# Five query tiles of the first attention split whole in scratch and placed by DMA, and the rotation of some tiles a tick or two earlier

## What is computed

```python
h = rms_norm(x, norm_mix_pre[l])
proj = h @ w_in[l]
qa, ka, va, qb, kb, vb = jnp.split(proj, SPLITS, axis=-1)
qa = apply_rope(rms_norm(qa.reshape(B, S, 8, 64), q_norm_a[l]), ang_axial)
ka = apply_rope(rms_norm(ka.reshape(B, S, 2, 64), k_norm_a[l]), ang_axial)
out_a = global_attention(qa, ka, va)            # every query sees every key
qb = apply_rope(qb.reshape(B, S, 8, 64), ang_1d)
kb = apply_rope(kb.reshape(B, S, 2, 64), ang_1d)
out_b = window_attention(qb, kb, vb, sink_b[l]) # three blocks of 128 keys, with a sink
# apply_rope: concatenate([x1 * cos - x2 * sin, x2 * cos + x1 * sin]) on the halves x1, x2 of a head
```

## Time and profile before

| | |
|---|---|
| median of three runs | 1161.18 us (1160.88 to 1161.55) |
| the profiled execution | 1164.91 us, its span 1163.1 us |
| TensorE's granted clock | 0.995 of full speed |
| PE busy | 1133.3 us (97% of the span) |
| DVE, ACT, POOL busy | 650.2, 503.0, 124.5 us |
| the attention of the first block (ticks 0 to 63) | about 43 to 175 us of the span |

### The profile page before, as it was taken

One profiled execution on the slowest core, in us unless ns is written; L12 is line 12 of the kernel. 1 busy time (PEld: TensorE's weight loads), 2 busy tenths in 40 slices (PEclk: granted clock), 3 DMA queues, 4 the chain that ended last, 5 costly groups with the idle time before them and its releaser, 6 DMA issues.

```text
span 1163.1 us, 15505 instructions
## 1 busy us (share of the span) xinstructions
PE 1133.3 (97%) x5560; PEld 936.3 (80%) x5560; DVE 650.2 (56%) x1085; ACT 503.0 (43%) x859; POOL 124.5 (11%) x143
## 2 busy tenths in 40 slices
PE   8999989999999999999999999999999999999997
PEld 6788767898888888888898887787888888888886
DVE  5888896966444444333378588563544444433333
ACT  5788885544223223222255458453322322332321
POOL 1476743000000000000000004200000000000000
PEclk8999999999999999999999999999999999999999
DMA  7321202213222222233223220032322222222312
GB/s 266 109 73 51 59 19 108 92 55 140 95 104 90 94 102 96 92 108 109 96 77 109 91 76 16 19 109 73 111 92 105 93 95 100 95 103 93 106 55 73
DMA packets 32515, 106.20 MB, mean 91 GB/s; under 512 B 4048, under 2 KB 6736, under 8 KB 32336
## 3 DMA queue, kind: packets, MB, share of 16 engines
q1 hardware_dynamic: 31712, 104.60, 25.5%
q10 hardware_dynamic: 752, 0.92, 0.3%
HBM read 100.78 MB, written 2.10 MB: 88 GB/s over the span
## 4 chain that ended last, share of the span: by engine, by line
PE 86%; DVE 6%; ACT 3%; POOL 2%; issue 2%; DMA 1%; ACTq 0%; SPq 0%; DVEq 0%; POOLq 0%
PE bank L502 24%; PE bank L504 24%; PE bank L503 23%; PE bank L1015 1%; PE bank L1005 1%; DVE wl L423 1%; PE bank L1088 1%; PE bank L963 1%; PE bank L964 1%; PE bank L965 1%; POOL pr L1335 1%; PE bank L1090 1%; PE bank L1089 1%; PE bank L2004 1%; PE bank L2002 1%
## 5 line engine op out<-in xcount | busy, mean ns | idle before, releaser
L423 DVE TENSOR_TENSOR wl<-raw,wh 128x1024 fp32r<-128x1024 f32 x181 | 223.9, 1238 | 299.3 <-ACT wh L415 299.2
L415 ACT ACTIVATE wh<-raw 128x1024 fp32r<-128x1024 f32 x181 | 191.1, 1057 | 420.3 <-PE bank L504 275.0
L502 PE MATMUL bank<-hh,wh 128*128 128x512 f32 x872 | 344.8, 395 | 4.3 <-DVE hl L1486 2.7
L504 PE MATMUL bank<-hh,wl 128*128 128x512 f32 x872 | 340.8, 391 | 0.0
L503 PE MATMUL bank<-hl,wh 128*128 128x512 f32 x872 | 340.6, 391 | 0.0
L502 PEld LDWEIGHTS bank<-hh,wh 128*128 128x128 f32 x872 | 164.4, 188 | 41.7 <-issue 4.8
L503 PEld LDWEIGHTS bank<-hl,wh 128*128 128x128 f32 x872 | 164.5, 189 | 35.3 <-issue 1.7
L504 PEld LDWEIGHTS bank<-hh,wl 128*128 128x128 f32 x872 | 164.2, 188 | 34.8
L504 PE MATMUL bank<-gh,wl 128*128 128x512 f32 x308 | 121.7, 395 | 0.0
L502 PE MATMUL bank<-gh,wh 128*128 128x512 f32 x308 | 121.7, 395 | 0.0
L503 PE MATMUL bank<-gl,wh 128*128 128x512 f32 x308 | 121.7, 395 | 0.0
(11 more groups left out here) (245 smaller groups left out, 1635.3 us busy)
## 6 DMA issues: line engine op xcount, KB each, us to landing
raw<-weights SPq DMA_DIRECT2D x181, 512.0 KB, 3.2
xres<-x_t SPq DMA_DIRECT2D x8, 512.0 KB, 7.6
sw<-ta SPq DMA_DIRECT2D x36, 64.0 KB, 2.0
out_t<-final SPq DMA_DIRECT2D x6, 256.0 KB, 2.5
rope<-angles SPq DMA_DIRECT2D x1, 1024.0 KB, 10.8
sw<-ta ACTq DMA_DIRECT2D x4, 64.0 KB, 3.1
wp<-pool_weights ACTq DMA_DIRECT2D x1, 256.0 KB, 2.6
out_t<-final ACTq DMA_DIRECT2D x1, 256.0 KB, 2.4
```

Source lines behind the costliest of these rows:

```text
L415: act.activation(wh[:, j, :, :], raw[:, j, :, :], ACT.Copy).then_inc(high_split, 1)
L423: v.tensor_tensor(wl[:, j, :, :], raw[:, j, :, :], wh[:, j, :, :].bitcast(F32), ALU.subtract)\
L502: pe.matmul(bank[:, :], wh[:, slot, b, :], ah[:, k, :], start=first and n == 0, stop=False)
L504: ins = pe.matmul(bank[:, :], wl[:, slot, b, :], ah[:, k, :], start=False, stop=last and n == len(blocks) - 1)
```

## The change

The whole split: for the tiles in `PLACED` ACT writes the high part of all 128 partitions into `sw`, DVE the low part of all 128 into `ta`, one instruction each instead of two of 64 partitions, and SP issues four DMAs for each tile (`place1`) which carry the two halves of `sw` and `ta` to the rows of `q1`: 20 DMAs of 128 KB more in all. They stand on SP one tick after the low part. PE's first scores of a head wait for that head's two DMAs (`placed[par]`). The scratch of a tile is taken up again only after its DMAs have landed (in `swap1` and in `vec_project1`).

The tables: `free` moves a step only off the ticks in which POOL really divides a head (t % 4 == 1, from 5), not off every odd tick. So COS, SIN, ADD or DONE of the tiles 4, 5, 6, 9, 10 and 11 come one or two ticks sooner (tile 7 stays). HIGH and LOW of the last five tiles are set anew.

| tile | COS | SIN | DONE | HIGH | LOW | first scores of its two heads in ticks |
|---|---|---|---|---|---|---|
| 4 before, after | 4, 3 | 6, 4 | 8, 7 | 10 and 11, same | 12, same | 16, 20 |
| 6 before, after | 14, 14 | 16, 15 | 16, 15 | 19 and 22, 19 | 21 and 24, 21 | 24, 28 |
| 7 before, after | 20, 20 | 22, 22 | 24, 24 | 26 and 28, 26 | 27 and 29, 27 | 32, 36 |
| 9 before, after | 32, 31 | 34, 32 | 34, 32 | 37 and 38, 34 | 38 and 39, 35 | 40, 44 |
| 10 before, after | 38, 38 | 40, 39 | 40, 39 | 43 and 45, 42 | 44 and 46, 43 | 48, 52 |
| 11 before, after | 44, 43 | 46, 44 | 46, 44 | 48 and 56, 48 | 49 and 57, 49 | 56, 60 |

```diff
 def free(t):
-    return t + 1 if t >= 3 and t % 2 else t
+    return t + 1 if t >= 5 and t % 4 == 1 else t

+PLACED = (6, 7, 9, 10, 11)
-LATER = {3: (4, 7), 4: (10, 11), 5: (16, 17), 6: (19, 22), 7: (26, 28), 9: (37, 38), 10: (43, 45), 11: (48, 56)}
+LATER = {3: (4, 7), 4: (10, 11), 5: (16, 17)}
+HIGH.update({(6, None): 19, (7, None): 26, (9, None): 34, (10, None): 42, (11, None): 48})
...
@@ pe_scores1
             if j == 0:
-                pe.wait_ge(f1.part.low, parted(tile1("q", qt), par))
+                if tile1("q", qt) in PLACED:
+                    pe.wait_ge(f1.placed[par], 32 * (PLACED.index(tile1("q", qt)) + 1))
+                else:
+                    pe.wait_ge(f1.part.low, parted(tile1("q", qt), par))
@@ vec_project1
+                    if p in PLACED:
+                        parts_placed(v, p)
@@ vec_part1
+            if m in PLACED:
+                v.tensor_tensor(ta[:, slot1(m), :].bitcast(F32R), src, sw[:, slot1(m), :], ALU.subtract).then_inc(f1.part.low, 1)
+                return
@@ act_part1
+            if m in PLACED:
+                act.activation(sw[:, slot1(m), :].bitcast(F32R), src, ACT.Copy).then_inc(f1.part.high, 1)
+                return
@@ new
+        def place1(eng, m):
+            r, idx, n = slot1(m), PLACED.index(m), Q_ORDER.index(IN1[m][2])
+            eng.wait_ge(f1.part.low, parted(m))
+            if n >= 4:
+                eng.wait_ge(at1.scores, 4 * head_at(Q_ORDER[n - 4], 1) + 4)
+            for par, own, other in pair():
+                if idx:
+                    eng.wait_ge(f1.placed[par], 32 * idx)
+                eng.dma_start(q1[own, n % 4, par, :].bitcast(F32), sw[own, r, :]).then_inc(f1.placed[par], 16)
+                eng.dma_start(q1[other, n % 4, par, :].bitcast(F32), ta[own, r, :]).then_inc(f1.placed[par], 16)
+        def parts_placed(eng, m):
+            for par in range(2):
+                eng.wait_ge(f1.placed[par], 32 * (PLACED.index(m) + 1))
@@ swap1
-            if p in EARLY1:
+            if p in PLACED:
+                parts_placed(eng, p)
+            elif p in EARLY1:
@@ sync
                     if t == SPLIT_LOW[m]:
                         load(0, m + 2 * RING, m % RING)
+                    if m in PLACED and t == LOW[m, None] + 1:
+                        place1(sp, m)
```

More of the change, by code:

```diff
@@ L160 @@
 DONE_ORDER = sorted((m for m in ROPED if m not in EARLY1), key=lambda m: (DONE[m], m))
+PLACED = (6, 7, 9, 10, 11)
 HIGH = {(m, 0): MIDDLE[m] + 1 for m in V_TILES}
 HIGH.update({(m, par): DONE[m] for m in EARLY1 for par in range(2)})
-LATER = {3: (4, 7), 4: (10, 11), 5: (16, 17), 6: (19, 22), 7: (26, 28), 9: (37, 38), 10: (43, 45), 11: (48, 56)}
+LATER = {3: (4, 7), 4: (10, 11), 5: (16, 17)}
 HIGH.update({(m, par): t for m in LATER for par, t in enumerate(LATER[m])})
+HIGH.update({(6, None): 19, (7, None): 26, (9, None): 34, (10, None): 42, (11, None): 48})
 LOW = {p: HIGH[p] + 1 if p[0] in ROPED else HIGH[p] for p in HIGH}
-LOW.update({(3, 1): 9, (4, 0): 12, (5, 1): 19, (6, 0): 21, (6, 1): 24})
+LOW.update({(3, 1): 9, (4, 0): 12, (5, 1): 19, (6, None): 21})
 KEYS = {m: LOW[m, 1] + (0 if m in EARLY1 else 1) for m in ROPED if IN1[m][1] == "k"}
-PARTED = sorted(HIGH, key=lambda p: (HIGH[p], p[0] in ROPED, p))
-assert PARTED == sorted(HIGH, key=lambda p: (LOW[p], p[0] in ROPED, p))
+PARTED = sorted(HIGH, key=lambda p: (HIGH[p], p[0] in ROPED, p[0], p[1] or 0))
+assert PARTED == sorted(HIGH, key=lambda p: (LOW[p], p[0] in ROPED, p[0], p[1] or 0))
 assert all(HIGH[m, 0] >= DONE[m] + 2 for m in LATER)
-assert all(COS[m] > LOW[ROPED[n], 1] for n, m in enumerate(ROPED[2:]))
+assert all(COS[m] > max(LOW[p] for p in LOW if p[0] == ROPED[n]) for n, m in enumerate(ROPED[2:]))
 def parted(m, par=None):
@@ L191 @@
 WHOLE = {i: 4 * head_at(i, 1) + OUT_LAG + 1 for i in range(8)}
-assert all(LOW[tile1("q", HEADS1[s][1]), HEADS1[s][2]] < 4 * s and KEYS[tile1("k", HEADS1[s][3])] < 4 * s for s in range(len(HEADS1)))
+assert all(max(LOW[p] for p in LOW if p[0] == tile1("q", HEADS1[s][1]) and p[1] in (None, HEADS1[s][2])) < 4 * s and KEYS[tile1("k", HEADS1[s][3])] < 4 * s for s in range(len(HEADS1)))
 SUM_A = STEPS + TURN1 - 1
@@ L838, in __init__ @@
                 self.part = Split("in1_parts")
+                self.placed = [sem(f"in1_placed{par}") for par in range(2)]
         f1 = First()
@@ L1139, in vec_tick @@
                     vec_rotate(v, m)
[L1140 to L1143, removed]
+            for m, par in PARTED:
+                if m in ROPED and t == LOW[m, par]:
+                    vec_part1(v, m, par)
             for m in ROPED:
@@ L1265, in act_tick @@
                     act.activation(esink[:, c], negm[:, c], ACT.Exp, bias=col("sink", aux)).then_inc(at1.sinks, 1)
[L1266 to L1269, removed]
+            for m, par in PARTED:
+                if m in ROPED and t == HIGH[m, par]:
+                    act_part1(act, m, par)
             for m in KEYS:
```

## The result

The changed kernel takes 1163.89 us (median of 15 runs, 1162.90 to 1165.66), the kernel before beside it 1161.60 us (15 runs, 1160.88 to 1163.46). The ratio is 1.0020, with a 95% interval of 1.0013 to 1.0027: slower by 2.3 us, just at the bound of what was called a difference. The forecast was 1162.1 us, inside a range of 1159.6 to 1164.9.

A forecast was written before the change was run, and what follows sets the result against it. PE was taken as the bound, busy 97% of the span, with room for gain only after 135 us. Early +2.7 and late -1.8 gave +0.9 us on the median 1161.18: 1162.1 us, range 1159.6 to 1164.9.

The forecast's parts named there:

- Sine and addition of tile 4: POOL, tick 4: put ahead of head 0's divisions, they make PE's first transposes 2.7 us late.
- The lower bound without blocking: Same place: if POOL never stands still behind DVE, the early delay is only +1.2 us.
- Carried unchanged by a full PE: PE, 60 to 135 us, busy 75.00 of 75.00 us: an earlier delay is not won back by 135.
- Divisions of head 7: POOL, tick 33: start moves from 118.98 to 120.4 us, hidden by 1.5 us of slack.
- Whole split, less work: Five instructions fewer each, 3.4 us of DVE and 3.1 of ACT; counts only where DVE is the bound.
- Placing DMAs: 20 DMAs on SP, 0.6 us an issue, 2.2 to land: cost nothing, slack 2 to 3 us or more.
- Ticks 35 to 44: Head 9's divisions start sooner, PE's idle time in tick 44 shrinks from 1.40 to 0.5 us: -0.9 us.
- Ticks 45 to 52: Head 10's divisions 0.3 us later, DVE eased behind them: -1.8 us in all by tick 52, the 0.9 included.
- Two of the signs named ahead: Ticks 48 to 52: scores' waits sum to 1 us or less; head 10's divisions follow tile 11's addition without idle time.
- The sign that was to decide: Prediction wrong if PE's scores of tick 52 come no sooner, measured from those of tick 36.
- late gain stays out: Rival, POOL 138 to 147 us: head 10's divisions after about 144.5, late gain only 0.3, 1163.6 us; chance 0.24.
- late gain whole: Rival, 135 to 156 us: all 4.1 us of PE's waits go, 1159.8 to 1158.3 us; chance 0.16.

The follow-up runs named there:

- e2: The kernel before with only tile 4's rotation sooner (COS 3, SIN 4, DONE 7): 1165.46 us, ratio 1.0034.
- e1: The changed kernel with tile 4's rotation back in its old ticks (COS 4, SIN 6, DONE 8): 1160.50 us, ratio 0.9993.
- e5: The changed kernel with DVE's split of tick 6 (weights of tile 8) moved to tick 8: 1163.22 us, ratio 1.0018.
- e12: e9 with only tiles 9, 10 and 11 split whole and placed, tiles 6 and 7 in halves as before: 1159.23 us, ratio 0.9981.
- e11: e9 with tile 9's high and low part in ticks 37 and 38 instead of 34 and 35: 1162.65 us, ratio 1.0005.
- e9: e1 with only tile 11's addition moved behind head 10's divisions (tick 46), its sine staying ahead: 1159.37 us, ratio 0.9983.
- e10: e9 with DVE's split of tick 48 moved to tick 55: 1159.13 us, ratio 0.9981.
- e6: e1 with DVE's split of tick 48 moved to tick 55: 1159.73 us, ratio 0.9988.
- e7: e4 with DVE's split of tick 48 moved to tick 55 and tile 11's high and low part one tick later: 1160.09 us, ratio 0.9989.
- e3: The kernel before with only the new rule for POOL's ticks, halves kept and no placing DMAs: 1166.01 us, ratio 1.0039.
- e4: The changed kernel with the rotations of tiles 4 and 11 back in their old ticks: 1161.15 us, ratio 0.9997.
- e13: The kernel before (halves, no placing DMAs) with e9's order on POOL: 1160.78 us, ratio 0.9995.

## Why the prediction was right, and where it was not

- **Sine and addition of tile 4: right.** Forecast +2.7, idle time 2.73, shift +2.61. The parts came as worked out: sine 1.73 and addition 2.19 us where an undisturbed one takes 1.28, then the divisions undisturbed, 2.69 (forecast 2.71). e2 shows it alone, e1 takes it away, e5 shows the blocking by the split. The lower bound without blocking (+1.2) is ruled out.
- **Carried unchanged by a full PE: right.** 64.27 against 64.34 us from the first transposes to tick 36.
- **Divisions of head 7: right.** Counted from PE's transposes of tick 36 they start 1.1 us later than before (forecast 1.4), and PE has no wait there. But the idle time before them (0.33 us) is ended by DVE's reciprocal: the collision that the forecast lacks stood here too, hidden by the slack.
- **Whole split, less work: right,** and by e12 the tiles 6 and 7 add nothing.
- **Placing DMAs: right,** no wait. e11 shows the price had they been late. The swap of tile 10 behind them came 1.2 us later, not 3.
- **Ticks 35 to 44: right.** Forecast -0.9, and PE's transposes of tick 44 come 0.97 sooner; their wait is 0.75 instead of 1.40 (forecast 0.5).
- **Ticks 45 to 52: the step that failed.** Forecast -1.8 in all, measured -0.9. DVE's split of tick 48 took 1.21 us as forecast (1.2), and tile 10's low part in tick 43 met no wait (0.71). I had POOL's addition of tile 11 delay only what stands behind it on POOL, and looked for collisions among DVE's large instructions alone. The addition met DVE's sum of head 10 with its four elements, which has both inputs in SBUF. DVE came second and stood for 1.1 us, and with it the reciprocal and the maximum behind it, for which PE then waited 1.30 us. The divisions lost only 0.3 us by it, since they stood behind the addition anyway. Two of the signs named ahead were missed: the scores' waits in ticks 48 to 52 sum to 2.5 us, not 1, and head 10's divisions have 0.33 us of idle time ended by DVE. The sign that was to decide, scores of tick 52 that come sooner counted from tick 36, came with 0.91 us. e9 moves this one instruction and finds 1.13 us: the gain is then 1.98, a little more than the 1.8 forecast.
- **The rival "late gain stays out"** had the right place (POOL, 138 to 147 us). The forecast's times for this stretch leave the early delay out; to compare with them, 1.04 us is added to the changed kernel's (its transposes of tick 36 stand at 122.07 instead of 123.11). Then the sine starts at 141.6 (forecast 141.3) and the divisions at 144.6, just past the 144.5 named as this rival's threshold (forecast 144.05): 0.3 us of it is the later swap, 0.3 the late reciprocal. So its condition was met, but what held PE's scores of tick 48 was DVE's maximum, which neither case names, and its 0.3 us of gain is below the measured 0.9. The rival "late gain whole" stays out also in e10: the maximum is not the only chain.

The Trainium skill (SBUF — State Buffer, section "Who interferes with whom") states that in such a pair whoever issues first holds the shared port and the other is fully blocked. The rows agree in both directions: POOL is blocked by DVE at 52.89 us (2.19 instead of 1.28), DVE by POOL at 142.02 (1.26 instead of 0.15). I had applied the rule in one direction only.

**The sum.** By the shift the change costs +1.72 us in its profiled execution, against +0.9 forecast; the 0.8 between is the failed step (0.9), less 0.1 by which the early part came out smaller. The medians differ by 2.3. What stands in the other 0.6 is open: no trace of the changed kernel shows it, but its runs fall into two groups, eight from 1162.90 to 1163.89 us with a mean clock of 0.997 to 0.999 and seven from 1164.39 to 1165.66 with 0.995 to 0.997. The profiled execution was of the first. Two falls of the clock are on record that have this size. One stands behind PE's stop of 2.73 us: the trace of e2 has it, it cost 1.2 to 1.5 us, and all six runs of e2 lie at 1165.25 to 1165.74. The other stands ahead of tick 1, before anything that was edited: the traces of e6, e7 and e11 have it, it cost 1.5 us, and all three belong to the upper runs of their kernels (e6: 1161.58 us, where eight of eleven lie at 1159.39 to 1159.95). The kernel before has runs of that kind as well, 2 of the 15 beside the changed kernel (1162.87 and 1163.46). Seven of 15 is more than that, which speaks for the first; that the upper group is made by it is not shown. That the forecast stands 1.8 us under the result is then 0.8 of the sum above, 0.6 that is put down to the clock, and 0.4 of the base (1161.18 in three runs, 1161.60 in fifteen).

So the number came out within its range, and by its size it is nearer to the rival "late gain stays out" (1163.6 us) than to the forecast's own 1162.1. The early part and the hidden parts were understood. That a missed collision, the clock and the base together stayed inside the range is in part luck.

## What to carry to other kernels

When an instruction of POOL that reads SBUF is moved, list what DVE runs beside its new place, down to the smallest instruction: with two SBUF inputs it stood here until POOL's was done, and everything behind it too, so the price was what was left of POOL's instruction (1.1 us) and not DVE's own 0.15. Less work is worth its time only where its engine is waited for, and a delay ahead of a stretch in which PE is never idle is paid in full. Two profiled executions are compared from a common event inside them, not by their spans: here the spans had even the wrong sign.

## What was not expected of the hardware

- A stop of TensorE of 2.73 us was followed by a granted clock of 0.55 and 0.60 over the next 4 us in one execution (e2), and by 1.00 in others with the same stop (the changed kernel, e3). In the late stretch e4 shows the same after 1.78 us (down to 0.50), and e13 after waits of 0.68 and 0.80 us. So one stop can cost once its length, and in some executions over a microsecond more. The Trainium skill (TensorE: Matmul & The Clock Gate, section "Part 1: The HAM clock gate") says that the gate follows how busy PE has been recently; the rows agree in kind, since each fall stands behind idle time. Why the same stop has the fall in one execution and not in another is left open here. Ahead of tick 1 it is the same: a clock of 0.50 behind a stop of 1.20 us in e6, and 1.00 behind one of 1.64 us in e9.
- DVE's addition of 128x4 took 0.15 us alone and 1.26 beside POOL's of 128x512 (in tick 33 1.25, in e1 1.24, in e9 again 0.15).
- Removing a collision moved it in e4 (DVE's split 2.30 us instead of 1.21), and the later split of e5 gave back 0.9 us at one place and took 0.7 at the next.
